# GpSimd subtracts weight chunks 0, 3, 6 and 9 of each expert instead of 2, 5, 8 and 11

## The reference, cut to what matters

```python
def swiglu(x, w_gu, w_down):
    g, u = jnp.split(x @ w_gu, 2, axis=-1)
    return (jax.nn.silu(g) * u) @ w_down
...
    for e in range(N_EXPERTS):
        out = out + gate_full[..., e:e + 1] * swiglu(x, w_gu[e], w_down[e])
```

## Time and profile before

| | |
|---|---|
| time, median of 3 runs | 1517.16 us (1513.23 to 1520.33) |
| the profiled execution | 1522.0 us, of it span 1520.3 us |
| PE busy / DVE / ACT / POOL | 1355.0 / 659.4 / 581.4 / 155.9 us |
| expert stage, from the first expert's products to the store of the last | about 1058 to 1408 us of the span |
| DMA, whole span | 172.33 MB, mean 113 GB/s |

### The profile page before, as it was taken

How to read it: one execution, slowest core, us unless ns; L and a number is a source line. 1 busy time by engine, 2 the same in 40 slices (tenths; PEclk the granted TensorE clock), 3 DMA queues, 4 the chain that set the end, 5 groups by cost and what they waited for, 6 DMA issues and landing times.

```text
span 1520.3 us, 17657 instructions
## 1 busy us (share of the span) xinstructions
PE 1355.0 (89%) x6511; PEld 1122.9 (74%) x6512; DVE 659.4 (43%) x927; ACT 581.4 (38%) x810; POOL 155.9 (10%) x114
## 2 busy tenths in 40 slices
PE   7999789799999999989899987977798999886378
PEld 6889777588888788858778976836696988775246
DVE  4332644633333323264423265445534433554463
ACT  3222633632323222163323233244545544664361
POOL 0000000000000000000000000001424333544100
PEclk9999889999999999999999987996999999997589
DMA  6323003133333423123365500205857755886301
GB/s 186 105 86 97 1 17 94 42 97 97 97 97 97 125 79 95 56 73 98 81 65 104 97 1 10 61 21 186 270 189 237 249 184 186 276 278 207 121 15 56
DMA packets 202666, 172.33 MB, mean 113 GB/s; under 512 B 7088, under 2 KB 186352, under 8 KB 202608
## 3 DMA queue, kind: packets, MB, share of 16 engines
q1 hardware_dynamic: 197616, 153.19, 35.9%
q0 software_dynamic: 4464, 16.25, 3.0%
q10 hardware_dynamic: 528, 2.10, 0.3%
HBM read 161.56 MB, written 9.96 MB: 113 GB/s over the span
## 4 chain that ended last, share of the span: by engine, by line
PE 76%; DVE 8%; issue 7%; ACT 4%; DMA 2%; POOL 2%; POOLq 0%; SPq 0%; ACTq 0%; DVEq 0%
PE bank L665 23%; PE bank L667 23%; PE bank L666 22%; PE bank L758 2%; POOL w_lo L627 1%; DMA y_dram<-y_tok,store_i 1%; DVE rstd L1598 1%; PE bank L827 1%; DVE w_lo L1514 1%; PE bank L831 1%; DMA x_tok<-x 1%; PE bank L972 1%; DVE sp L1699 0%; ACT x_exact L1232 0%; PE bank L889 0%
## 5 line engine op out<-in xcount | busy, mean ns | idle before, releaser
L1514 DVE TENSOR_TENSOR w_lo<-raw,w_hi 128x1024 fp32r<-128x1024 f32 (+5 forms) x219 | 304.0, 1394 | 317.8 <-ACT w_hi L1164 165.8
L665 PE MATMUL bank<-x_hi,w_hi 128*128 128x512 f32 x736 | 291.4, 396 | 23.7 <-DVE x_lo L1514 19.4
L666 PE MATMUL bank<-x_lo,w_hi 128*128 128x512 f32 x736 | 289.4, 393 | 0.0
L667 PE MATMUL bank<-x_hi,w_lo 128*128 128x512 f32 x736 | 289.1, 393 | 0.0
L1164 ACT CAST w_hi<-raw 128x1024 fp32r<-128x1024 f32 (+2 forms) x141 | 149.7, 1063 | 166.2 <-PE bank L667 159.0
L665 PE MATMUL bank<-w_hi,x_hi 128*128 128x256 f32 (+2 forms) x608 | 191.9, 316 | 18.5 <-issue 10.3
L666 PE MATMUL bank<-w_lo,x_hi 128*128 128x256 f32 (+2 forms) x608 | 189.2, 311 | 0.0
L667 PE MATMUL bank<-w_hi,x_lo 128*128 128x256 f32 (+2 forms) x608 | 189.1, 311 | 0.0
L665 PEld LDWEIGHTS bank<-x_hi,w_hi 128*128 128x128 f32 x736 | 139.8, 190 | 60.4 <-issue 17.9
L667 PEld LDWEIGHTS bank<-x_hi,w_lo 128*128 128x128 f32 x736 | 139.9, 190 | 29.7
L666 PEld LDWEIGHTS bank<-x_lo,w_hi 128*128 128x128 f32 x736 | 140.2, 190 | 28.4
(11 more groups left out here) (256 smaller groups left out, 1819.0 us busy)
## 6 DMA issues: line engine op xcount, KB each, us to landing
raw<-moe_w_gu SPq DMA_DIRECT2D x32, 768.0 KB, 5.2
raw<-ffn_w_gu SPq DMA_DIRECT2D x44, 512.0 KB, 3.8
raw<-moe_w_gu SPq DMA_DIRECT2D x32, 640.0 KB, 4.2
raw<-a_w_qkv SPq DMA_DIRECT2D x24, 512.0 KB, 3.6
raw<-moe_w_down SPq DMA_DIRECT2D x16, 768.0 KB, 5.7
raw<-ffn_w_down SPq DMA_DIRECT2D x16, 704.0 KB, 4.6
raw<-ple_w_gate SPq DMA_DIRECT2D x16, 512.0 KB, 4.1
raw<-kvf_w SPq DMA_DIRECT2D x16, 512.0 KB, 7.9
```

The lines of the kernel that those rows point to most:

```text
L665: pe.matmul(o, s_hi, m_hi, start=start, stop=False, skip_group_check=True)
L666: pe.matmul(o, s_hi, m_lo, start=False, stop=False, skip_group_check=True)
L667: return pe.matmul(o, s_lo, m_hi, start=False, stop=stop, skip_group_check=True)
L1514: return dve.tensor_tensor(dst, a, b, ALU.subtract)
```

## The change

POOL takes chunks 0, 3, 6 and 9 (`c % 3 == 0`) and DVE the other eight. In POOL's list the subtraction of 12, chunk 0 of the next expert, is the last before the store, and the subtraction of chunk 3 is the first after it. The gather stands between chunks 3 and 6. The additional 64x512 rest of the down weights is done by POOL for chunk 9 and by DVE for chunk 11. The counts follow. Before the loop POOL subtracts chunk 0 of the first expert, which DVE did at the end of `proj1`, and DVE subtracts chunk 2.

```diff
 def is_third(c):
-    return c % 3 == 2
+    return c % 3 == 0
...
 def others_count(e, c):
-    return L0 + 8 * e + c - c // 3 + 1
+    return L0 + 8 * e + c - c // 3
...
             def gate1_step(q, i, j, last):
                 c = RAW * i + j
-                if c < RAW or c == RAW + 2:
+                if c <= RAW:
                     raw_free(NE, c)
                 else:
-                    sp_eng.wait_ge(lo_ready, L0 + 8 * NE + max(c - RAW, c - RAW + (c < RAW + 2)))
+                    sp_eng.wait_ge(lo_ready, L0 + 8 * NE + c - RAW)
...
                 op = pool.tensor_tensor(w_lo[j][:, 0:n], raw[j][:, 0:n], w_hi[j][:, 0:n].bitcast(F32), ALU.subtract)
-                if c == 11:
+                if c == 9:
...
             gather(0, 1)
-            third_low(0, 2)
+            third_low(0, 0)
             with experts(nc, pool) as e:
-                third_low(e, 5)
+                third_low(e, 3)
                 pool.wait_ge(xg_turned, TT * e + TT)
                 gather(e + 1, 2 * e + 2)
-                third_low(e, 8)
-                third_low(e, 11)
-                third_low(e, 14)
+                third_low(e, 6)
+                third_low(e, 9)
+                third_low(e, 12)
...
                 def step(q, i, j, last):
-                    ahead(name, q, j, last)
+                    if layer == 0 or not last:
+                        ahead(name, q, j, last)
...
                 op = minus(w_lo[j][:, 0:n], raw[j][:, 0:n], w_hi[j][:, 0:n].bitcast(F32))
-                if c == 9:
+                if c == 11:
...
             deep_lo(0, 1)
             x_low(0, count(0))
+            deep_lo(0, 2)
             with experts(nc, dve) as e:
                 here, after = count(e), count(e + 1)
                 until_turned(e, here)
                 x_low(e + 1, after)
-                for c in (12, 13):
+                for c in (13, 14):
                     deep_lo(e, c)
```

More of the change, by code:

```diff
@@ L673, in weights @@
                     pe.wait_ge(lo_ready, 4 * q + j + 1)
-                elif c == 2:
-                    pe.wait_ge(third_lo_ready, third_count(NE, 2))
+                elif c == 0:
+                    pe.wait_ge(third_lo_ready, third_count(NE, 0))
                 else:
-                    pe.wait_ge(lo_ready, L0 + 8 * NE + c + (c < 2))
+                    pe.wait_ge(lo_ready, L0 + 8 * NE + c)
             def expert_weights(e, c):
```

## The result

The changed kernel takes 1541.42 us (median of 4 runs, 1538.91 to 1545.95) against 1518.74 (4 runs, 1513.23 to 1521.83): a ratio of 1.0157, 95% interval 1.0117 to 1.0196, about 24 us slower. The forecast was 1535, 18 us over the median then known. The result lies 1.4 us above the forecast's own range (1527 to 1540) and inside the range for 8 in 10 (1521 to 1545), which took in the clock's case. The profiled executions, with spans of 1520.3 and 1537.2 us, differ by 16.9; single executions of one kernel lie up to 8.6 us apart, as the four of before show. So single steps are compared stage by stage here, and whole kernels by their ratios.

The account below looks back on a forecast made before the run. PE's work bounds experts 1, 3 and 4, a ring of load, cast, subtraction and next load the others. 6.6 + 6.6 + 4.0 + 3.2 - 1.8 = 18.6, about +18 on 1517.16: 1535 us; range 1527 to 1540, 8 in 10 1521 to 1545.

Parts of the forecast that it names:

- the clock's case: Rival: PE granted half speed in chunks 9 and 10, 4.0 us more in two of experts 2, 5, 6; 1543; chance 0.15.
- the gain that it took for the end: After expert 7: last store issued 1.78 us after ACT's copy at 1400.78 instead of at 1404.38, -1.8 us.
- the clear loss: Whole kernel above 1524.7 us: all of the forecast, the half-speed clock rival and a third of a 1523 us rival, 0.83.
- The stall at chunk 3: Experts 2, 5, 6, 7: POOL subtracts chunk 3 only after the store's landing; PE gets it 5.0 to 5.1 us late.
- The earlier issue: Store after one-tile experts goes 1.78 us after the copies, 2.1 us earlier in expert 5; nothing gained after two-tile experts.
- From chunk 3 to chunk 9: One-tile experts: way from chunk 3's subtraction to chunk 9's product takes 20.6 us, against 19.1, 21.6 and 22.4 in experts 5, 6, 7.
- something that would prove a step wrong: Signs against: chunk 3 waits under 2 us, DVE's subtraction of 7 doesn't queue behind POOL, or stores land in under 3 us.
- 1.35 us of port wait: DVE's chunk 7 queues behind POOL's chunk 6 on the shared port, ending 1.35 us after POOL.
- the equal of expert 5: Expert 2 taken as losing the same as expert 5: 5.1 + 1.5 = 6.6 us.
- Expert 7: Loses 5.0 us at chunk 3, less 1.8 on the way to chunk 9: 3.2 us.

Follow-up runs that it names:

- The later store: Changed kernel with three fills of unused buffers on POOL between its wait for the copies and the store, delaying its issue: 1545.36 us, ratio 1.0178 to the kernel before.

## Why the prediction was right, and where its sizes were off

It was right in direction, mechanism and place. The size is 4 (by the medians) to 5 us (by the ratio) over its sum of 18.6, with the gain that it took for the end missing (1.8) and the clock's case, kept apart as a rival, partly come true beside it. The chances for the clear loss, as it lists them, add up to 0.85 and not to the 0.83 that it names. Its steps against the trace, in us (forecast; then experts 5, 6 and 7, where a step has them):

| step | forecast | measured |
|---|---|---|
| last copy to the store's issue, one tile | 1.78 | 1.49, 1.49, 1.49 |
| issue to landing, one tile | 5.24 | 6.41, 5.88, 5.44 |
| POOL's chunk 3 | 3.49 | 4.10, 3.41, 3.82 |
| PE's wait at chunk 3 | 5.1, 5.0, 5.0 | 5.9, 6.1, 5.9 |
| chunk 3 to the load of 11 | 8.4 | 7.4, 7.5, 7.3 |
| load of 11 to its cast | 7.5 | 6.4, 6.8, 6.2 |
| end of that cast to chunk 9's product | 3.0 | 4.1, 4.0, 4.4 |
| chunk 3 to chunk 9, sum | 20.6 | 19.5, 19.9, 19.5 |
| chunk 9 to the last copy | 7.75 | 9.6, 9.5, 9.6 |
| last copy to landing, end of expert 7 | 5.1 (from 7.0) | 6.9 |

**The stall at chunk 3** is the term that carries the result. The run that gave the chunk back to DVE took away 19 of 24 us, and the run that moved only the wait 11. It was mis-sized by some 1 us each: in expert 5 POOL's subtraction took 4.10 where I took 3.49, because DVE's subtraction of chunk 5, new in that place, had begun at 1303.85, just before it; in 6 because the landing grew, in 7 by both (5.88 and 3.82).

**The earlier issue** was the step that failed. I took 2.1 us off for the store of a one-tile expert and 1.8 at the end, with the landing unchanged. The issue did come 2.4 us sooner after the copies (3.86 to 1.49), the landing only 1.2 in expert 5 (9.1 to 7.9), and at the end 0.0. The later store showed why: it shares the DMA engines with the load sent just before it.

**From chunk 3 to chunk 9** came out within 1.1 us in experts 5, 6 and 7, by errors that cancel. The gather took 2.7 us, not 3.9 (1349.49 to 1352.15), so DVE's chunk 7 didn't queue behind POOL: in expert 6 it began 0.2 us after chunk 6's end and took 1.49. That was named as something that would prove a step wrong, and that step, 1.35 us of port wait, is wrong here. The wait for the port is seen elsewhere: POOL's 64x512 rest of chunk 9 took 2.79 us beside DVE's chunk 10 and 1.28 alone, and DVE's chunk 11 took 2.49. In expert 2 alone of the four, where POOL gathers two tiles, chunk 7 queued (2.77 us). There the way took 22.6 us, 1.9 more than before, so it was not quite the equal of expert 5 that the prediction took it for. Against that, the way from the cast of 11 to chunk 9 was a microsecond longer: in expert 6 DVE's chunk 10 and its product for the hidden came first, so that 11 began 0.3 us after its cast and took 2.49, and PE began 0.7 us after the low half.

**The clock.** In the profiled executions PE was granted half speed in a part of the stretch behind chunk 9's first product in experts 2, 5, 6 and 7 after the change, and only in 7 before. It costs 1.3, 1.8 and 1.7 us in 2, 5 and 6 and gives 2.1 back in 7 (11.76 to 9.63), where half speed now lasts less. The rival forecast 4 us in each of two experts: it came true, in half its size, beside the forecast's case. The later store's trace has 4 us in each of 5 and 6. Within one kernel the clock goes with the time: of 21 executions of the kernel before, timed together, the fastest had 1509.75 us at a mean granted clock of 0.948, the slowest 1524.94 at 0.937. How much of the 24 us is the clock's is open, since the mean also falls while PE stands waiting.

**Expert 7** lost 0.7 us, not 3.2: up to chunk 9's first product it lost 2.8, and 2.1 came back by the clock. **Expert 1** is 3.5 us shorter after, which no step foresaw. Its first product came 1.4 us after the last copy and not 3.4, with less half clock behind it; in the runs with POOL at 2, 5, 8 and 11 that wait varied (2.1 to 4.1 us of PE's idle time) and with POOL at 0 it was always 1.9 to 2.1. Why is open.

The eight experts together come to +20.1 us in the two traces, where the forecast was 20.4 before the end's 1.8. Up to chunk 9's first product the agreement is the mechanism's, with the cancelling errors told above: 7.6, 6.1, 4.1 and 2.8 us (20.6) stand against 6.6, 6.6, 4.0 and 3.2. That the totals agree too is luck: the clock's 2.7 and 0.4 in expert 0 happen to be made up by expert 1's 3.5. The medians differ by 22.7 us and not by 16.9 as the profiled executions do; what the rest is, no trace shows.

## What to carry to other kernels

A wait for a transfer's landing is a barrier for its whole engine: look at what stands first behind it, and give that place to work that is needed last, or move the wait to the operation that really needs the landing (here the gather, which writes where the stored rows lie). Ask of a moved piece of work who follows it in order, not only who waits for it: SP's loads went out in the order of the chunks, so one late subtraction held back the loads of three chunks (7, 8 and 9). A store that is issued 2.4 us earlier gained 1.2 us and, at the end, nothing, where it only joined the loads on the DMA queues. And before two traces are compared, look at the granted clock: stretches in which PE was busy throughout differed by 4 us between two executions of one kernel.

## What the runs showed of the hardware

- An indirect store of one tile (0.52 MB) landed 3.35 to 3.38 us after its issue in experts 5 to 7 of the runs with the store issued later or ahead of 14, where SP's last load was 2.5 us old or more. In the kernel after it took 5.4 to 6.4 where SP had issued a load of 0.52 or 0.66 MB a microsecond before, and 7.4 in expert 0, where the load was issued 0.2 us before. Issued 1.4 us later, expert 5's landed 1.7 us sooner after the copies (6.2, not 7.9). The estimate from the Trainium skill (DMA: Bandwidth & Descriptors, section Anatomy of one DMA — SWDGE (gpsimd) path), 3.2 us, comes near only where no load was in the way.
- Subtractions of DVE and POOL from and to SBUF held each other up where they overlapped, in either order: behind DVE, POOL's 64x512 rest took 2.79 us and not 1.28, and its 1536 columns 4.10 and not 3.5; behind POOL, DVE's 1280 columns took 3.79 us before the change and 4.59 in the run with the later store, and not 1.49.
- PE's granted clock was at half (1.2 GHz) for a part of the stretch behind chunk 9's first product in experts 5 to 7, after waits of 2.6 to 3.0 us ahead of the transposes and 1.5 to 1.9 at chunk 9, following the 6 us at chunk 3; before, with waits of 0.7 and 1.1 in expert 5, it stood at full speed there. The waits need not differ by much: with the wait ahead of the gather and POOL at 2, 5, 8 and 11, expert 5 had full speed in the trace with waits of 1.0 and 1.5 us, and half speed for most of the stretch in the one with 2.1 and 1.3.
